# Norm sums of one stacked transformer kernel: squares added on VectorE, or taken by TensorE pair by pair

## The reference, cut to what matters

```python
def rmsnorm(x, g):
    xf = x.astype(jnp.float32)
    y = xf * lax.rsqrt(jnp.mean(xf * xf, axis=-1, keepdims=True) + EPS)
    return (y * g.astype(jnp.float32)).astype(x.dtype)

def first_block(x, mem, ...):
    for layer in range(DEPTH):          # DEPTH = 2
        h = h + mixer(rmsnorm(h, ...))              # even_mixer, then conformer_conv
        h = h + cross_attn(rmsnorm(h, ...), mem, ...)
        h = h + feed_forward(rmsnorm(h, ...))       # swiglu, then 8 experts
    return rmsnorm(h, final_norm)
```

## Time and profile before

| | us |
|---|---|
| median of 3 runs | 2520.29 |
| lowest and highest | 2519.24, 2521.05 |
| the profiled execution, its own time | 2526.12 |
| its span in the trace | 2524.3 |
| TensorE matmuls busy in the span | 2372.9 (94%) |
| VectorE busy | 693.2 (27%) |
| ScalarE busy | 379.8 (15%) |

### The profile page before, as it was taken

How to read it: one execution, slowest core, us unless ns; L and a number is a source line. 1 busy time by engine, 2 the same in 40 slices (tenths; PEclk the granted TensorE clock), 3 DMA queues, 4 the chain that set the end, 5 groups by cost and what they waited for, 6 DMA issues and landing times.

```text
span 2524.3 us, 34254 instructions
## 1 busy us (share of the span) xinstructions
PE 2372.9 (94%) x14906; PEld 1354.0 (54%) x14906; DVE 693.2 (27%) x1476; ACT 379.8 (15%) x812; POOL 54.1 (2%) x70
## 2 busy tenths in 40 slices
PE   7899999998989999989998999988979998989997
PEld 6777888877577333333333333335756335756433
DVE  2565122149665101011010101011142121263122
ACT  1101100010111111101110111102032111153212
POOL 0000000025000000000000000000000000000000
PEclk9899999999999999999999999998989999989998
DMA  9488154553366898999999999998412997532591
GB/s 320 171 300 312 67 212 155 197 208 120 114 223 225 300 388 324 389 370 392 395 394 392 394 394 358 388 370 319 158 42 72 323 342 170 147 121 72 190 347 48
DMA packets 328741, 645.09 MB, mean 256 GB/s; under 512 B 12907, under 2 KB 98177, under 8 KB 328577
## 3 DMA queue, kind: packets, MB, share of 16 engines
q1 hardware_dynamic: 325804, 637.63, 70.3%
q10 hardware_dynamic: 2773, 5.11, 0.6%
HBM read 641.66 MB, written 1.05 MB: 255 GB/s over the span
## 4 chain that ended last, share of the span: by engine, by line
PE 86%; DVE 8%; issue 3%; ACT 2%; ACTq 0%; DVEq 0%
PE bank L1598 22%; PE bank L1296 17%; PE bank L1663 11%; PE bank L1563 6%; PE bank L1517 6%; DVE att L3296 4%; PE bank L1529 3%; PE bank L1590 3%; PE bank L1316 3%; PE bank L1723 2%; PE bank L1682 1%; PE bank L1342 1%; PE bank L1649 1%; PE bank L1809 1%; PE bank L1743 1%
## 5 line engine op out<-in xcount | busy, mean ns | idle before, releaser
L1598 PE MATMUL bank<-ring,xn 128*32 128x512 f32 x3648 | 468.7, 594 | 0.0
L1296 PE MATMUL bank<-xn,ring 128*128 128x256 f32 x2048 | 453.5, 383 | 3.1 <-ACT xn L2225 1.1
L1296 PEld LDWEIGHTS bank<-xn,ring 128*128 128x128 f32 x2048 | 392.2, 192 | 62.1 <-issue 8.7
L1598 PEld LDWEIGHTS bank<-ring,xn 128*32 128x32 f32 x3648 | 128.4, 110 | 272.9 <-issue 269.2
L1663 PE MATMUL bank<-ring,att 128*32 128x512 f32 x2256 | 254.4, 593 | 1.3 <-ACT att L2346 1.3
L2903 DVE TENSOR_TENSOR sq<-att,bank 32x512 f32<-32x512 f32 x70 | 48.0, 686 | 501.2 <-ACT att L2357 352.3
L1563 PE MATMUL bank<-ring,xn 128*64 128x512 f32 x304 | 145.9, 627 | 28.6 <-issue 28.6
L1663 PEld LDWEIGHTS bank<-ring,att 128*32 128x32 f32 x2256 | 72.8, 110 | 162.5 <-issue 162.1
L1517 PE MATMUL bank<-xn,ring 128*128 128x256 f32 x704 | 152.8, 379 | 0.0
L1565 PE MATMUL bank<-ring,xn 128*64 128x512 f32 x304 | 146.7, 629 | 0.0
L1517 PEld LDWEIGHTS bank<-xn,ring 128*128 128x128 f32 x704 | 133.8, 190 | 18.3
(11 more groups left out here) (354 smaller groups left out, 2214.3 us busy)
## 6 DMA issues: line engine op xcount, KB each, us to landing
ring<-od_moe_gu SPq DMA_DIRECT2D x98, 2048.0 KB, 17.7
ring<-od_moe_down SPq DMA_DIRECT2D x49, 2048.0 KB, 16.4
ring<-ada_w SPq DMA_DIRECT2D x24, 2048.0 KB, 8.7
ring<-moe_w_gate SPq DMA_DIRECT2D x32, 1024.0 KB, 10.7
ring<-moe_w_up SPq DMA_DIRECT2D x32, 1024.0 KB, 10.4
ring<-moe_w_down SPq DMA_DIRECT2D x16, 2048.0 KB, 13.8
z<-od_moe_gu SPq DMA_DIRECT2D x14, 2048.0 KB, 18.9
ring<-ev_w_in SPq DMA_DIRECT2D x10, 2048.0 KB, 19.7
```

The costliest lines, as they stand in the source:

```text
L1296: mm = nc.tensor.matmul(ps[:, c * T:(c + 1) * T], kblk(b)[:, k, u * T + c * P:u * T + (c + 1) * P], x[:, k, :], start=k == 0, stop=k == KD ...
L1598: return nc.tensor.matmul(PSB[f.b][j * QP:(j + 1) * QP, :], src[:, k, at:at + QP], kblk(b)[:, k, :], start=k == 0, stop=k == KD - 1)
```

## The change

In eleven of the twelve stages VectorE no longer adds squares. TensorE opens the norm's bank first and issues 5 products of zeros into that bank (10 before, into bank 7), then one product of zeros over the 2 columns of the result, and then, for each pair of chunks that ScalarE has squared, four products by the column of `mean_of`, all accumulated: 16 products, which are 32 records, in place of 4 products and 8 records. `norm_mem` keeps its additions. `add_squares` does nothing in the eleven stages.

```diff
-        def sum_of(st):
-
-            st.sum, st.spread, st.added = count(sum_ready, 1), count(spread_ready, 1), 0
+        def sum_of(st, raw=True):
+
+            st.raw, st.spread, st.added = raw, count(spread_ready, 1), 0
+            st.sum = None if raw else count(sum_ready, 1)
...
-            sum_of(st)
+            sum_of(st, to_xn)
...
+            def busy_in(f, n):
+
+                ps = open_bank(f)
+                for _ in range(n):
+                    nc.tensor.matmul(ps, no_bits, zero_row, start=True, stop=True)
...
-            def pe_mean_squares(st, n=10):
-                busy(st.idle, n)
-                pe.wait_ge(sum_ready, st.sum + 1)
-                ps = open_bank(st.fill)
-                for c in range(TC):
-                    for j in range(2):
-                        mm = nc.tensor.matmul(ps[:, c:c + 1], sq[:, j, c * P:(c + 1) * P], mean_of[:, 0:1],
-                                              start=j == 0, stop=j == 1)
+            def pe_mean_squares(st, n=5):
+                busy_in(st.fill, n)
+                ps = PSB[st.fill.b]
+                if st.raw:
+                    nc.tensor.matmul(ps[:, 0:TC], no_bits, no_bits[:, 0:TC], start=True, stop=False, skip_group_check=True)
+                    for k in range(KD):
+                        if k % 2 == 0:
+                            pe.wait_ge(sq_ready, st.sq + k // 2 + 1)
+                        for c in range(TC):
+                            mm = nc.tensor.matmul(ps[:, c:c + 1], sq[:, k, c * P:(c + 1) * P], mean_of[:, 0:1],
+                                                  start=False, stop=k == KD - 1, skip_group_check=True)
+                else:
+                    pe.wait_ge(sum_ready, st.sum + 1)
...
-            def pe_norm(st, n=10):
+            def pe_norm(st, n=5):
...
-                while st.added < upto:
+                while not st.raw and st.added < upto:
```

More of the change, by code:

```diff
@@ L1349, in spread_roots @@
                 mm.then_inc(done, 1)
-            def pe_mean_squares(st, n=10):
-                busy(st.idle, n)
-                pe.wait_ge(sum_ready, st.sum + 1)
-                ps = open_bank(st.fill)
-                for c in range(TC):
-                    for j in range(2):
-                        mm = nc.tensor.matmul(ps[:, c:c + 1], sq[:, j, c * P:(c + 1) * P], mean_of[:, 0:1],
-                                              start=j == 0, stop=j == 1)
+            def pe_mean_squares(st, n=5):
[11 more added lines that the diff above has]
+                    pe.wait_ge(sum_ready, st.sum + 1)
+                    for c in range(TC):
+                        for j in range(2):
+                            mm = nc.tensor.matmul(ps[:, c:c + 1], sq[:, j, c * P:(c + 1) * P], mean_of[:, 0:1],
+                                                  start=j == 0, stop=j == 1)
                 mm.then_inc(bank_full[st.fill.b], 1)
```

## The result

| | before | after |
|---|---|---|
| median of 6 runs | 2520.43 us | 2543.42 us |
| lowest and highest | 2515.88, 2524.60 | 2540.60, 2546.27 |
| the profiled execution, its own time | 2526.12 | 2545.63 |
| its span | 2524.3 | 2543.8 |
| mean granted clock of TensorE | 0.966 | 0.957 |

The changed kernel is slower: the ratio of the times is 1.009, with a 95% interval of 1.0076 to 1.0104. Between the medians that is +23.0 us, between the two profiled executions +19.5. They differ because the profiled execution of before stands 5.7 us above its median, and above the highest of its six runs, and that of after 2.2 above its own.

A forecast was written before the change was run, and what follows sets the result against it. TensorE's matmuls, 86% of the chain, bound the kernel. Terms 6.5 + 0.7 + 11.9 - 2 + 4.5 + 1.5 + 1.1 = +24.2 us gave 2544.5 us (2550.3 profiled), own range 2533 to 2554, stated range 2529 to 2557.

The forecast's parts named there:

- not given back: Ahead of the first experts: the delay is not recovered, because their weight loads move with the slots TensorE frees.
- The record part: Six plain norms: 32 records take 3.63 us; with fewer zeros and no wait, +6.5 us together, clock aside.
- "As it comes" hides nothing: Plain norms: TensorE finishes the earlier layer first and takes the squares in a row behind it, never waiting for the last.
- the rival of a gain: Changed norms: products hide behind the squares, only the last four follow the last square; -16 us, 2504; chance 0.04.
- The clock term: Six plain norms and `conv`: the clock falls in each, 7 x 1.7 = +11.9 us.
- a fall costs half of the 3.41 us, so 1.7 us: Plain norms and `conv`: price of one clock fall, from the slow stretch at line 1818; bounds 0 and 3.4.
- the rival of a held clock: Changed norms keep the clock, by the skill's rule; +4.2 us, or +7.0 with `od2` slow anyway; about 2526; chance 0.14.
- The third rival: Each clock fall lasts about twice as long because the 32 records keep it low; +39.5 us, 2560; chance 0.14.
- The end of the range at -5.1: `norm_od`: gain if the clock holds, mean ending at 527.1 in place of 531.20; taken was -2, other end 0.
- the two bounds: `norm_ev`: 32 records take 3.63 us at full clock (-0.2) or 7.13 at half (+3.3); taken +1.5.
- VectorE's freed additions are worth nothing: Changed norms: 33 freed additions, 22.8 us of VectorE work, gain nothing beyond the other terms, as VectorE idles there.

## Why the prediction was right, point by point

**The sign and the size** were right: forecast +24.2, measured +23.0 between medians. That it came so near is in part luck, for two reasons. The measured norms sum to +24.1 from terms that missed on both sides: the clock in the six plain norms and `conv` was too cheap by 4.7 us, and `norm_od`, `norm_ev` and `final2` too dear by 4.6. And in the traces, where the difference is +19.5, some 6.6 us came back between the layers, which is below, under "not given back".

**The record part** was right. Zeros to the start of the records take 285.36 - 284.25 = 1.11 us (1.13 forecast), and the 32 records 3.71 us where the clock holds (3.63 forecast, from a line with two columns). With the zeros between the records the part alone comes out at 0.9 to 1.0 us per norm, and at the one expert norm where the clock held over dead records at 1.0, against 1.05.

**"As it comes" hides nothing** was right in the plain norms: no wait stands inside any group of line 1367 there. In `norm_od` and `norm_ev`, which the rival of a gain had on its side, the pairs did overlap with the squares, and both came out at the better end of their ranges.

**The clock term was mis-sized.** The step "a fall costs half of the 3.41 us, so 1.7 us" took the length from line 1818, where it fell behind the records. In the changed norms the zeros ahead put the fall amid the records, and in five of the six plain norms and `conv` the slow stretch is 6.8 us long. Per norm the clock then costs 2.7 us, not 1.7; over the six plain norms (20.8 - 6.5) / 6 = 2.4 us, the last with a single stretch of 3.4. That it fell at all, in seven of seven, was right, and the rival of a held clock (2526) is out. The third rival, 3 us for each fall, had the better price for the plain norms and failed on the others.

**`conv`** cost +3.0 against +2.4: the same cause, a slow stretch of 6.8 us from 674.0.

**`norm_od`, `norm_ev`, `final2`** were too dear, by 2.1, 1.4 and 1.1 us. In `norm_od` I feared a fall within the records, which the window shows did not come: 32 records in 3.71 us, and the mean ends 4.81 us after the zeros began (4.76 forecast). The end of the range at -5.1 was the nearer one. In `norm_ev` the 32 records took 4.26 us, closer to the 3.63 than to the 7.13 of the two bounds; but that row moves by 1.4 us between executions, so its miss of 1.4 says little. `final2` kept its clock through its records.

**`od2`** was right: +4.3 against +4.5, 32 records at the lower level in 6.97 us (7.13 forecast), and the idle time ahead of it 4.48 us as before (4.28).

**"Not given back" was wrong as a general statement.** Ahead of the first experts it held (+0.1 over the 900 us behind). But 6.3 us went between `od2` and the last experts, where I had looked for nothing. The prediction took the idle time without a releaser to be fixed, naming only that ahead of `od2` as what could prove it wrong; the runs show that it moves with the place of the code, at `twin` (+2.0) as at `od2`. How much came back is known less well than 6.3: the trace of before is a slow execution, 5.7 us above its median, and its slow stretch at 2162.90 is in neither of the two kernels compared with it above. Between medians the changed kernel lost 3.5 us more than between traces, so about that much of the 6.3 may belong to that one execution.

**"VectorE's freed additions are worth nothing"** was right. With the additions kept and 24 dead records added, the first plain norms cost the same as in the change.

What stays open: why the packets of the instruction queue come late behind a skipped block, and why there is idle time behind `od2` in some kernels and none in others. No run separates what in the records lowers the clock, the one column, the f32 type or the weight load with each; and `cross1` without zeros ahead and the first expert norm with dead records kept 2.4 GHz over 32 of them, so they do not always do it. The medians of the run with dead records stand 10 us further from before than its profiled execution, which was not traced.

## What to carry to other kernels

Moving a reduction from an idle VectorE to a TensorE that bounds the kernel pays only for the part that runs before the last input is there; count how many of the products fit between the end of TensorE's own work and the last input (here four records of 32). Long rows of one-column f32 products cost twice: their own time, and then the clock for several us, with no gap to be seen. And when a change moves instructions around skipped conditional blocks, compare the idle rows without a releaser, and the packets of the instruction queue beside them, before a difference of a few us is put down to the edit: here 24 products that never run made a stop of 5.8 us where there had been none.

## What was new about the hardware

- One-column f32 records in a row can lower TensorE's clock although it is fully busy: 32 of them were followed by 6.8 us at 1.2 GHz in five of the six plain norms and by 3.4 in the sixth, and 24 dead and 8 live by 6.8 in four. Groups of eight with four zeros of 512 columns between them kept 2.4 GHz in five of the six.
- A single 128x128 record with one column takes 3.71 / 32 = 0.116 us at full clock and 6.97 / 32 = 0.218 at half.
- Slow stretches of 3.4 us cost a norm 0.9 to 1.4 us and ones of 6.8 us 2.3 to 2.7, less than half of their length. That part of such a norm waits for VectorE and ScalarE would explain it, but no run tests this.
- Behind a skipped conditional block TensorE stands 4.3 to 5.5 us without a releaser, and in many kernels a second time, for up to 7.7 us, some instructions later. Where the second stop falls depends on where the code lies, and 50 of 50 such stops ended 1.3 to 1.9 us after a 16 KB packet of the queue that the profile calls `instruction`.
